# Products of the identity with itself on TensorE ahead of 33 of its waits

## The reference, cut to what matters

```python
def first_block(x, ...):            # twice
    h = rmsnorm(x, norm1_g[i]);  z = h @ w_in[i] + b_in[i]
    # mLSTM and retention heads on z, each gated, then
    merged = sigmoid(gm) * (y_m @ w_bm[i]) + sigmoid(gr) * (y_r @ w_br[i])
    x = x + merged @ w_out[i]
    x = x + square(relu(rmsnorm(x, norm2_g[i]) @ w_ff1[i] + b_ff1[i])) @ w_ff2[i] + b_ff2[i]
    x = x + sigmoid(rmsnorm(x, norm3_g[i]) @ w_pe_gate[i]) * (p[i] @ w_pe[i])
...
def second_block(x, ...):           # layer 0: even_mixer (GLA, RWKV-7), layer 1: dsa_mixer
    for layer in range(DEPTH):
        mix = even_mixer(x, ...) if layer % 2 == 0 else dsa_mixer(x, ...)
        x = layer_norm(DN_ALPHA * x + mix, mix_ln_g[layer], mix_ln_b[layer])
        ffn = peer_ffn(x, ...)      # every expert's hidden value, gated by a top-k
        x = layer_norm(DN_ALPHA * x + ffn, ffn_ln_g[layer], ffn_ln_b[layer])
```

## Time and profile before

| | us |
|---|---|
| three runs | 3479.33, 3479.53, 3483.65 |
| median | 3479.53 |
| the profiled execution's time | 3481.0 |
| its span, from the first to the last instruction | 3479.2 |

### The profile page before, as it was taken

One profiled execution on the slowest core, in us unless ns is written; L12 is line 12 of the kernel. 1 busy time (PEld: TensorE's weight loads), 2 busy tenths in 40 slices (PEclk: granted clock), 3 DMA queues, 4 the chain that ended last, 5 costly groups with the idle time before them and its releaser, 6 DMA issues.

```text
span 3479.2 us, 49014 instructions
## 1 busy us (share of the span) xinstructions
PE 3227.4 (93%) x20420; PEld 2853.3 (82%) x20420; DVE 2170.7 (62%) x3106; ACT 1501.7 (43%) x1713; POOL 567.4 (16%) x282
## 2 busy tenths in 40 slices
PE   7899999988999998977999999999868999999998
PEld 7787789786877896876999989888658989889886
DVE  5665655556656555675886755555676967645555
ACT  5443454454444544612434444444334444444443
POOL 0000000000000000000667610000112766400000
PEclk8999999989999999988999999999979999999999
DMA  5355545424446453403443365555423533565553
GB/s 189 132 184 184 194 162 189 168 101 152 175 162 222 158 189 133 178 7 106 169 159 140 133 232 198 183 192 184 167 73 139 177 138 138 188 222 186 184 192 121
DMA packets 87670, 565.15 MB, mean 162 GB/s; under 512 B 10176, under 2 KB 10192, under 8 KB 23584
## 3 DMA queue, kind: packets, MB, share of 16 engines
q1 hardware_dynamic: 80496, 534.81, 43.0%
q0 software_dynamic: 6960, 27.27, 2.4%
HBM read 552.60 MB, written 9.44 MB: 162 GB/s over the span
## 4 chain that ended last, share of the span: by engine, by line
PE 45%; DVE 6%; POOL 4%; ACT 3%; issue 1%; DVEq 0%; ACTq 0%
PE bank L1891 7%; PE bank L1892 7%; PE bank L1893 7%; PE bank L1870 6%; PE bank L1872 6%; PE bank L1871 6%; POOL w_lo L1519 3%; ACT w_hi L2015 2%; PE bank L1853 1%; POOL hot_j L1536 1%; PE bank L1613 1%; PE bank L1615 1%; PE bank L1614 1%; PE bank L1589 1%; PE bank L1590 1%
## 5 line engine op out<-in xcount | busy, mean ns | idle before, releaser
L2015 ACT ACTIVATE w_hi<-raw 128x2048 fp32r<-128x2048 f32 x291 | 557.1, 1915 | 818.4 <-PE bank L1893 395.7
L2292 DVE TENSOR_TENSOR w_lo<-raw,w_hi 128x2048 fp32r<-128x2048 f32 x216 | 505.8, 2342 | 590.3 <-ACT w_hi L2015 590.3
L908 DVE TENSOR_TENSOR w_lo<-raw,w_hi 128x2048 fp32r<-128x2048 f32 x201 | 460.0, 2292 | 399.3 <-ACT w_hi L713 398.1
L1870 PE MATMUL bank<-act_hi,w_hi 128*128 128x256 f32 x2048 | 591.3, 289 | 30.4 <-POOL w_lo L1519 24.9
L713 ACT ACTIVATE w_hi<-raw 128x2048 fp32r<-128x2048 f32 x201 | 384.3, 1915 | 531.9 <-PE bank L483 370.5
L1871 PE MATMUL bank<-act_lo,w_hi 128*128 128x256 f32 x2048 | 579.2, 283 | 0.0
L1872 PE MATMUL bank<-act_hi,w_lo 128*128 128x256 f32 x2048 | 579.0, 283 | 0.0
L1870 PEld LDWEIGHTS bank<-act_hi,w_hi 128*128 128x128 f32 x2048 | 392.0, 191 | 36.1 <-POOL w_lo L1519 29.9
L1519 POOL TENSOR_TENSOR w_lo<-raw,w_hi 128x2048 fp32r<-128x2048 f32 x75 | 355.2, 4740 | 405.1 <-ACT w_hi L2015 239.3
L1891 PE MATMUL bank<-w_hi,c_hi 128*128 128x512 f32 x1024 | 405.0, 396 | 0.0
L1892 PE MATMUL bank<-w_lo,c_hi 128*128 128x512 f32 x1024 | 405.0, 395 | 0.0
(11 more groups left out here) (496 smaller groups left out, 5711.4 us busy)
## 6 DMA issues: line engine op xcount, KB each, us to landing
raw<-weights SPq DMA_DIRECT2D x492, 1024.0 KB, 4.8
row<-rows POOLq DMA_DIRECT2D x48, 256.0 KB, 4.4
spill<-staged SPq DMA_DIRECT2D x32, 256.0 KB, 3.4
hid<-spill SPq DMA_DIRECT2D x32, 256.0 KB, 4.9
y<-w_pe POOLq DMA_DIRECT2D x2, 1024.0 KB, 5.0
ln_row_mix<-ln_rows POOLq DMA_DIRECT2D x4, 512.0 KB, 4.7
hid<-keys POOLq DMA_DIRECT2D x2, 1024.0 KB, 6.5
ln_row_ffn<-ln_rows POOLq DMA_DIRECT2D x4, 512.0 KB, 7.5
```

Of the source, the lines that this page charges most:

```text
L908: nc.vector.tensor_tensor(w_lo[:, k % SPLIT, :], raw[:, k % RAW, :], w_hi[:, k % SPLIT, :].bitcast(F32), ALU.subtract).then_inc(lo_ready, 1)
L1870: mm(dst, wh[:, ws], act_hi[:, kk_, :], start=kk_ == 0 and jj == 0, stop=False)
L2015: A.activation(hi_of(k), raw[:, k % RAW, :], ACT.Copy).then_inc(hi_ready, 1)
L2292: V.tensor_tensor(lo_of(k), raw[:, k % RAW, :], hi_of(k).bitcast(F32), ALU.subtract).then_inc(lo_ready, 1)
```

## The change

`warm(bank, n)` issues n fp32 products of the identity (stationary) with the identity repeated four times (moving, 512 columns) into a bank that is free there. It is called ahead of a wait, 248 products in all when the program is run; in `transposes` of the second block 69 products have 256 columns instead. In all there are 33 groups: ten in each layer of the first block (6, 9, 13, 4, 6, 3, 6, 3, 5 and, at the layer's end, 12 or 18), and in the second block 8, 8, 15, 13, then 11 and 11, 16 and 13 (256 columns), 13, 27, 24, and 11 and 7 (256 columns). At the end of a layer a wait for the reader of `peg`'s first bank comes before them. Nothing is removed.

```diff
+            wide_ident = ident.unsqueeze(1).broadcast_to([P, CW // P, P])
+            def warm(bank, n):
+                for _ in range(n):
+                    nc.tensor.matmul(psum[bank][:, :], ident, wide_ident, start=True, stop=True)
...
-                def nat(name, i, hi, lo, ready=None, tiles=None, half=None):
+                def nat(name, i, hi, lo, ready=None, tiles=None, half=None, warmth=0):
                     if tiles is None or 0 in tiles:
                         bank_free(CHUNK[name, i])
+                        warm(2 * (CHUNK[name, i] % 2), warmth)
...
-                feat("mqk", 1, act_hi, act_lo)
+                feat("mqk", 1, act_hi, act_lo, warmth=6)
...
+                warm(4, 9)
                 pe.wait_ge(m_ready, 1 + layer * A_LAYER["m_ready"])
...
-                nat("mv", 1, act_hi, act_lo)
+                nat("mv", 1, act_hi, act_lo, warmth=13)
...
                     between(1, 1)
+                    warm(4, warmth)
                     outputs(3)
...
-                nat("gm", 1, act_hi, act_lo, tiles=(0,))
+                nat("gm", 1, act_hi, act_lo, tiles=(0,), warmth=6)
...
-                nat("bm", 0, mix_hi, mix_lo, by_bank(T_YM))
+                nat("bm", 0, mix_hi, mix_lo, by_bank(T_YM), warmth=3)
...
+                nat("rg", 3, act_hi, act_lo, warmth=6)
...
+                warm(4, 3)
                 normed(1)
...
+                warm(4, 5)
                 normed(2)
...
                 nat("peg", 1, act_hi, act_lo, half=half_done)
+                wait_read(pe, CHUNK["peg", 0], layer)
+                warm(2 * (CHUNK["peg", 0] % 2), 18 if layer else 12)
...
         def transposes(src, ready=None, warmth=(0, 0)):
             for t in range(TT):
                 if ready is not None:
+                    for _ in range(warmth[t]):
+                        mm(psum[4][:, :].rearrange("p (k s) -> p k s", k=2)[:, :, HALVES[t]], ident, wide_ident[:, 0:2, :], start=True, stop=True)
                     pe.wait_ge(x_ready, normed(ready, t))
...
+        warm(6, 8)
         pe.wait_ge(even_dve, EVEN_DVE["states"])
...
         for n in range(LEVELS):
             for t in range(TT):
+                if t and n == 0:
+                    warm(1, 8)
                 by_dve(f"d{n - 1}" if n else "lr", t)
...
                 direct(0)
+                warm(4, 15)
             pe.wait_ge(chain_dve, 2 * n + 1)
...
+        warm(1, 13)
         pe.wait_ge(rw_out, TT)
...
-            transposes(x, 2 * layer)
+            transposes(x, 2 * layer, (11, 7) if layer else (11, 11))
...
-        transposes(x, 1)
+        transposes(x, 1, (16, 13))
...
+        warm(4, 13)
         pe.wait_ge(odd_dve, ODD_DVE["turned"])
...
+        warm(6, 27)
         pe.wait_ge(odd_dve, ODD_DVE["rope"])
...
+        warm(6, 24)
         for t in range(TT):
             for hh in range(2):
                 turn_weights(t, hh)
```

More of the change, by code:

```diff
@@ L536, in bank_free, with feat @@
                         wait_read(pe, c - 2, layer)
-                def nat(name, i, hi, lo, ready=None, tiles=None, half=None):
+                def nat(name, i, hi, lo, ready=None, tiles=None, half=None, warmth=0):
                     if tiles is None or 0 in tiles:
                         bank_free(CHUNK[name, i])
+                        warm(2 * (CHUNK[name, i] % 2), warmth)
                     natural(base, TILE[name, i], CHUNK[name, i], PER_CHUNK[name], hi, lo, ready, tiles, half)
-                def feat(name, i, hi, lo, ready=None):
+                def feat(name, i, hi, lo, ready=None, warmth=0):
                     bank_free(CHUNK[name, i])
+                    warm(2 * (CHUNK[name, i] % 2), warmth)
                     featured(base, TILE[name, i], CHUNK[name, i], hi, lo, ready)
@@ L606, in _, with attend @@
                 nat("mv", 0, act_hi, act_lo)
-                nat("mv", 1, act_hi, act_lo)
-                def attend(h0, width, values, qk_ready, v_chunk, y_read, between):
+                nat("mv", 1, act_hi, act_lo, warmth=13)
+                def attend(h0, width, values, qk_ready, v_chunk, y_read, between, warmth=0):
                     def outputs(h):
@@ L648, in _ @@
                 attend(0, MDV + 1, lambda t, h: val_m[:, t, h, :], mqk_ready, CHUNK["mv", 1], my_read,
-                       lambda i, j: nat("mo", i, act_hi, act_lo, tiles=(j,)))
+                       lambda i, j: nat("mo", i, act_hi, act_lo, tiles=(j,)), warmth=4)
                 nat("gm", 0, act_hi, act_lo)
-                nat("gm", 1, act_hi, act_lo, tiles=(0,))
+                nat("gm", 1, act_hi, act_lo, tiles=(0,), warmth=6)
                 pe.wait_ge(y_ready, 2 + layer * A_LAYER["y_ready"])
@@ L662, in _ @@
                        lambda i, j: nat("rg", i, act_hi, act_lo, tiles=(j,)))
-                for i in range(2, 4):
-                    nat("rg", i, act_hi, act_lo)
+                nat("rg", 2, act_hi, act_lo)
+                nat("rg", 3, act_hi, act_lo, warmth=6)
                 nat("gr", 0, act_hi, act_lo)
@@ L1572, in halves_of, with warm @@
                 pe.wait_ge(tr_lo, split + ki // 2 + 1)
+        wide_ident = ident.unsqueeze(1).broadcast_to([P, CW // P, P])
+        def warm(bank, n):
+            for _ in range(n):
+                mm(psum[bank][:, :], ident, wide_ident, start=True, stop=True)
         def natural(name, i, tiles=(0, 1), split=None, half=None):
@@ L1616, in featured, with transposes @@
                 last.then_inc(tile_used, 1)
-        def transposes(src, ready=None):
+        def transposes(src, ready=None, warmth=(0, 0)):
             for t in range(TT):
                 if ready is not None:
+                    for _ in range(warmth[t]):
+                        mm(psum[4][:, :].rearrange("p (k s) -> p k s", k=2)[:, :, HALVES[t]], ident, wide_ident[:, 0:2, :], start=True, stop=True)
                     pe.wait_ge(x_ready, normed(ready, t))
```

## The result

The changed kernel took 3528.5 us (median; 3524.3 to 3530.6) where the kernel before took 3479.6: a ratio of 1.0135, with a 95% interval of 1.0122 to 1.0148. It is 49 us slower; 36 us were forecast (3516 us, with a range of 3496 to 3540). The profiled execution has a span of 3527.4 us, 48.2 more than before.

A forecast was written before the change was run, and what follows sets the result against it. TensorE was taken to bound the kernel, with its clock to be regained. Overrun 91 us, less 15 absorbed, less 59 - 19 of clock return, gave +36 us: 3516 us forecast, range 3496 to 3540, chance 0.76.

The forecast's parts named there:

- what is absorbed: Overrun of the groups that later waits or cancelling clock returns take up, at input gates, norms, queries and weights: 15 us.
- the returns that are lost in a later wait: Time regained from the clock but only waited for again, at several places in both blocks: 19 us of 59.
- The price: Each added 512-column identity product is two records, 0.86 us; 256 columns cost 0.43; all groups together 243 us.
- The half clock comes back: Full clock replaces half clock in 26 stretches with 131.8 us of TensorE work; 45% returns, 59 us at most.
- queries and weights: Second block, 27 products before the rotated queries and 24 before the attention weights: TensorE 15.9 us late, some +13 us.
- rounds of the solve and the chain behind them: Eight products in a 1.37 us wait of round 0 lose 5.4 us in full; with the chain, +8 us.
- end of the first block's second layer (18 products): 18 products, 15.5 us, stand in a wait of 8.8 us: +5 us.
- the ordinary layer of the first block comes out near zero: First block: overruns of some 15 us meet returns of some 12 and what waits for DVE absorb.
- The fills fit: Rival: one record, 0.43 us, per product, so groups nearly all fit their waits; -38 us, 3442 us; chance 0.08.
- The clock does not come back: Rival: identity products do not hold the clock, or begin at half clock; overrun alone gives 3557 us or more; chance 0.08.
- its second leg: The Trainium skill's rule that TensorE transposes do not count as clock activity; if so, 3557 us or more would follow.
- More is absorbed: Rival: TensorE's lateness meets DVE-set waits at twice as many places and returns are kept; +11 us, 3491 us; chance 0.08.

The follow-up runs named there:

- the same, again: The changed kernel run once more without any edit, for its first 50 us: 3523.2 us (the profiled execution) and 3530.4 us.
- twice as many: The changed kernel with twice as many identity products in every group: 3770.6 us, ratio 1.0828 to the kernel before.
- half: The changed kernel with half as many identity products in every group, rounded down: 3458.0 us, ratio 0.9928 to the kernel before.
- quarter: The changed kernel with a quarter of the identity products in every group, rounded down: 3478.4 us, ratio 0.9990 to the kernel before.
- transposes: The changed kernel with four identity transposes for each 512-column product and two for each of 256: 3461.2 us, ratio 0.9944 to the kernel before.
- fitted: Changed kernel with identity transposes sized to each wait, the solve's group one step later, four more waits given groups: 3446.2 us, ratio 0.9899 to the kernel before.
- fitted, more places: The fitted kernel plus transposes at the start, norms and gates' logarithms, and 16 more ahead of the attention weights: 3439.7 us, ratio 0.9879 to the kernel before.

## Why the prediction was right, and where it was too small

Each trace gives four terms. The groups' work is added up from start to start. The overlap is how long a group's first record starts before the modelled end of the record ahead of it (some 0.15 us each). The idle time filled is that of the kernel before (251.8 us) less that of the run. The clock's return is how much less than 3227.4 us TensorE is busy outside the groups. The work less the other three is the change of the span.

| kernel | work | overlap | idle filled | returned | span | clock |
|---|---|---|---|---|---|---|
| forecast | 243 | 5 | 143 | 59 | +36 | 0.98 to 0.99 |
| changed kernel | 241.5 | 5.0 | 141.6 | 46.7 | +48.2 | 0.989 |
| the same, again | 239.9 | 5.1 | 141.6 | 51.1 | +42.2 | 0.992 |
| twice as many | 486.4 | 5.0 | 141.0 | 50.1 | +290.3 | 0.991 |
| half | 121.3 | 5.0 | 102.0 | 34.5 | -20.3 | 0.986 |
| quarter | 58.2 | 4.4 | 53.2 | 4.4 | -3.9 | 0.975 |
| transposes | 130.3 | 5.0 | 108.2 | 40.2 | -23.1 | 0.988 |
| fitted | 156.1 | 5.7 | 133.9 | 54.7 | -38.2 | 0.993 |
| fitted, more places | 173.9 | 7.1 | 149.0 | 59.6 | -41.8 | 0.995 |

The forecast's 143 is 147 + 15 - 19: the waits, what is absorbed, and the returns that are lost in a later wait.

- **The price** (0.86 us, two records): right, 241.5 us against 243, and by itself 242 against 243.
- **The idle time filled**: right, 141.6 us in both executions against 143. The 33 waits are gone whole (147.1 us), and later waits are 5.5 us longer, where the forecast had 4 (lost less absorbed; the sum shows only their difference). Nearly all of it is 0.6 us at each of ten waits behind transposes.
- **The half clock comes back**: right as a mechanism, and the term that was too large: 46.7 us and 51.1 in two executions against 59. What half clock costs was right. The prediction took 131.8 us of work at half clock to be gone, and 45% of that to come back. Outside the groups TensorE is busy at half clock for 157.0 us in the kernel before, and still for 57.0 us in the changed kernel (47.0 in the second trace), so 100.0 and 110.0 us are gone; 45% of that is 45 and 50. The stretches at half did not go whole. Behind the group ahead of `mrow`, for instance, the clock was at half from 72.7 to 83.0 us; in the changed kernel it is at full behind the group and then at half from 83.9 to 87.3 us, so that 3.4 of those 10.3 us are left.

By place, from how much later the same product starts than before, each time for the last one ahead of a place's first group and ahead of the next place's (for the 18 products up to the large products behind them):

| place | forecast | measured | the same, again |
|---|---|---|---|
| queries and weights | +13 | +13.4 | +13.5 |
| rounds of the solve and the chain behind them | +8 | +8.9 | +8.7 |
| end of the first block's second layer (18 products) | +5 | +5.4 | +5.4 |
| the second block's other groups | in the rest (+10) | +10.3 | +10.3 |
| first 50 us | near zero | +3.8 | -2.2 |
| first block's two layers but for these | near zero | +6.3 | +6.5 |

The rest of +10 is what the forecast's 36 leave beside the three named places. The three add up to 27.7 us of the 48.2 and came within 1 us each.

The step that failed is "the ordinary layer of the first block comes out near zero": overruns and returns do not cancel there. The largest part is at the second chunk of `mv`, where 13 products make TensorE 4.1 us later in the first layer and 3.8 in the second, and the return behind them takes back only 1.7 and 1.6; the end of the first layer (12 products) adds 1.8. These 6 us are in both traces. The 3.8 us in the first 50 us are in the first trace alone. Of the six executions of the changed kernel two were traced, at 3529.2 and 3523.2 us; three others took 3527.8 to 3530.6 and one 3524.3, so the median probably lies with those that have it.

The signs named ahead came as well: 496 and 138 records, no idle time behind the groups, the second round 5.6 us later against the first (5 forecast), the turned weights 2635.15 - 2611.83 = 23.3 us behind the second logits (23), DVE idle for 6.34 us at L2813 (6). TensorE comes to the turned weights (2635.15 - 2584.12) - (2583.93 - 2548.77) = 15.9 us late, as worked out. Its busy share is 97% and not 98.

**The rivals.** "The fills fit" gave 3442 us for a price of 0.43 us. The price was wrong, but the runs with half the work are this case, and they show its size: 3458 us with half, since such groups leave 20 stretches at half clock (34.5 us returned, with 33 stretches in the kernel before), and up to 14.3 us of the return are waited for again or met by an overrun (some 2 of them are the solve's group, which is too long for its wait even at half). With groups fitted to their waits the return is 54.7 us, up to 16.5 of them are waited for again, and the span falls by 38.2. That this is just what the rival gave (-38, with 59 and 19 and an overrun of 1.9) is partly luck: the fitted groups stand at four more places. "The clock does not come back" falls with the clock of 0.989, and its second leg with the run of transposes. "More is absorbed" falls: the waits that are left grew by 5.5 us in all, and for this rival they would have had to shrink.

## What to carry to other kernels

Filling a wait to hold TensorE's clock pays only as long as the filling ends before its wait: within it, it cost nothing here, and each microsecond beyond it was a microsecond on the path. So price the filling from a row of the same type and form (plain fp32 products here are two records, not one), fit each group to its own wait with the smallest piece at hand so that it ends close to the wait's end (with some 2 us left open and a shorter wait behind them, the clock fell in two of the places above), and look which of two neighbouring waits is the long one. And of the time that the clock gives back, expect less at the end of the kernel: here up to 17 of 55 us only made TensorE wait longer for an engine that had not become faster.

## What the runs showed of the hardware

- Transposes of an fp32 identity held the granted clock as well as products did: 0.988 against 0.986 at a like length of groups, and 0.993 to 0.995 where they filled nearly every wait.
- How much of a wait is left open bears on what runs at full behind it: after 11.3 us of products and 1.99 us of idle time eight transposes ran at full clock, and then, after 0.88 us more of idle time, it was granted as 0.50; after 5.3 us and 8.00 us of idle time they ran at half. With 0.41 us left open ahead of the weights instead of 2.17, the transposes that had run at half ran at full.
- Two executions of one program differ by 6.0 us, all of it in the first 50 us, where one was granted 0.78 and the other 0.96 of full clock; 3.9 of them stand ahead of the first added product. A gain of that size in a median of four runs says little, and the timeline at the place says more.
